# A two-layer hybrid transformer trunk on one core: where TensorE computes the modulation rows

## The reference

```
mx = (silu(c) @ w_mod[i] + b_mod[i])          # w_mod[i] is 1024 x 6144, six rows of 1024
sh1, sc1, g1, sh2, sc2, g2 = split(mx, 6)
x = x + g1 * mixer(modulate(rms_norm(x, norm1_g[i]), sh1, sc1))
x = x + g2 * moe_ffn(modulate(rms_norm(x, norm2_g[i]), sh2, sc2), ...)
```

## Time and profile before

| | |
|---|---|
| median of 3 runs | 909.59 us |
| profiled execution | 907.71 us, span 905.8 us |
| TensorE busy | 833.9 us (92%), 6940 products |
| VectorE, ScalarE, GpSimd busy | 406.6, 241.3, 93.1 us |
| DMA | 300.59 MB, mean 332 GB/s |
| chain that ended last | TensorE 66%, DMA 17%, VectorE 8% |
| mean granted TensorE clock | 0.961 |
| one VectorE addition of 128x512 (line 1459) | 689 ns |

### The profile page before, as it was taken

One profiled execution on the slowest core, in us unless ns is written; L12 is line 12 of the kernel. 1 busy time (PEld: TensorE's weight loads), 2 busy tenths in 40 slices (PEclk: granted clock), 3 DMA queues, 4 the chain that ended last, 5 costly groups with the idle time before them and its releaser, 6 DMA issues.

```text
span 905.8 us, 16815 instructions
## 1 busy us (share of the span) xinstructions
PE 833.9 (92%) x6940; PEld 520.8 (57%) x6940; DVE 406.6 (45%) x674; ACT 241.3 (27%) x449; POOL 93.1 (10%) x162
## 2 busy tenths in 40 slices
PE   5898999999999799999996999989899899998994
PEld 2588995596646355553543887467555355453541
DVE  0468998737422222332336643466622232332334
ACT  3742435613211011111103523343111111110112
POOL 4184000012000000000000254100000000000000
PEclk9999999997999799999997999999999899999998
DMA  9999996848999999989997986596999999989993
GB/s 357 367 259 295 333 355 192 289 164 286 368 392 397 392 397 391 389 274 399 394 398 294 328 240 184 172 382 225 385 391 397 389 398 393 392 304 393 392 397 131
DMA packets 142158, 300.59 MB, mean 332 GB/s; under 512 B 12576, under 2 KB 43584, under 8 KB 142072
## 3 DMA queue, kind: packets, MB, share of 16 engines
q1 hardware_dynamic: 135360, 286.53, 87.5%
q0 software_dynamic: 6384, 12.76, 4.9%
q10 hardware_dynamic: 328, 0.11, 0.0%
HBM read 291.77 MB, written 2.92 MB: 325 GB/s over the span
## 4 chain that ended last, share of the span: by engine, by line
PE 66%; DMA 17%; DVE 8%; issue 3%; ACT 3%; SPq 2%; DVEq 0%; ACTq 0%
PE ps L2016 20%; DMA ring<-in_moe_w 11%; PE ps L2041 11%; PE ps L1969 4%; DMA ring<-in_w_mod 4%; PE ps L2106 3%; PE ps L1939 3%; DMA ring<-in_na_w_in 2%; PE ps L1940 2%; PE ps L1620 2%; PE ps L2132 2%; PE ps L2134 2%; PE ps L2133 2%; SPq L621 2%; DVE wlo L1106 2%
## 5 line engine op out<-in xcount | busy, mean ns | idle before, releaser
L2016 PE MATMUL ps<-ring,xg 128*64 128x256 f32 (+1 forms) x2432 | 255.3, 394 | 11.1 <-DMA ring<-in_moe_w 9.7
L2016 PEld LDWEIGHTS ps<-ring,xg 128*64 128x64 f32 (+1 forms) x2432 | 134.3, 130 | 103.2 <-issue 41.2
L1475 DVE SCALAR_TENSOR_TENSOR xres<-ps,gs,xres 128x512 f32<-128x512 f32 x128 | 90.0, 747 | 188.4 <-PE ps L1969 188.4
L2041 PE MATMUL ps<-ring,hidT 128*64 128x512 f32 (+1 forms) x608 | 121.8, 607 | 7.5 <-DMA ring<-in_moe_w 6.7
L2041 PEld LDWEIGHTS ps<-ring,hidT 128*64 128x64 f32 (+1 forms) x608 | 33.0, 129 | 76.6 <-issue 63.2
L1106 DVE TENSOR_TENSOR wlo<-ring,whi 128x1024 fp32r<-128x1024 f32 x56 | 66.6, 1219 | 12.8 <-ACT whi L807 12.8
L807 ACT CAST whi<-ring 128x1024 fp32r<-128x1024 f32 x56 | 56.8, 1045 | 53.0 <-DMA ring<-in_na_w_in 37.0
L1459 DVE TENSOR_TENSOR yg<-ps,g2keep 128x512 f32<-128x512 f32 x32 | 21.5, 689 | 82.7 <-PE ps L2041 82.7
L1620 PE MATMUL ps<-ring,pair 128*32 128x256 f32 x576 | 45.6, 436 | 12.6 <-DMA ring<-in_w_mod 7.7
L974 ACT COPY xg<-ps 128x384 f32<-128x384 f32 (+2 forms) x44 | 20.7, 470 | 130.7 <-PE ps L1940 130.7
L1939 PE MATMUL ps<-pick,hthi 128*128 128x192 f32 (+1 forms) x192 | 50.3, 302 | 0.0
(11 more groups left out here) (265 smaller groups left out, 1323.7 us busy)
## 6 DMA issues: line engine op xcount, KB each, us to landing
ring<-in_moe_w SPq DMA_DIRECT2D x384, 512.0 KB, 11.7
ring<-in_w_mod SPq DMA_DIRECT2D x96, 512.0 KB, 7.3
ring<-in_na_w_in SPq DMA_DIRECT2D x24, 512.0 KB, 8.7
ring<-in_cf_pw_w SPq DMA_DIRECT2D x24, 512.0 KB, 8.4
ring<-in_ab_w_out SPq DMA_DIRECT2D x8, 512.0 KB, 4.9
mods<-mod_scratch POOLq DMA_DIRECT2D x8, 512.0 KB, 7.1
urep<-uT SPq DMA_DIRECT2D x64, 35.5 KB, 3.5
urep<-uT POOLq DMA_DIRECT2D x64, 35.5 KB, 3.4
```

Source lines behind the costliest of these rows:

```text
L1475: V.scalar_tensor_tensor(out=dst, in0=ps[:, plan.spread_banks(m, i)[half], :], scalar=gs[:, t, place:place + 1], in1=dst, op0=ALU.mult, op ...
L2016: ins = T.matmul(ps[lo:lo + width, BW[a], c0:c0 + 2 * P], tile[:, k, o:o + width], raw[:, p.slot(u), w0:w0 + 2 * P], start=(q == 0 and kk ...
L2041: ins = T.matmul(ps[lo:lo + width, BY[a], :], hidT[:, a, o:o + width], raw[:, p.slot(u), half * HALF:(half + 1) * HALF], start=(q == 0), s ...
```

## The change

The arithmetic stays as it is; the order does not.

- `FIRST`: the 24 units of modulations 5, 6 and 7 stand among the output projection's 8 units, three ahead of each, instead of 16 among them and 8 behind. In the attention TensorE takes one unit in even turns and two in odd ones. Bank 7 holds modulation 7.
- `SECOND`: modulation 9 stands behind the second unit of pw2, ahead of the next four; 10 and 11 behind these; the last two units of pw2 at the end. TensorE takes modulation 9 (into bank 1) ahead of pw1's last block, and all of 10 and 11 behind the last convolution, ahead of pw2. The last piece of `cuts` is 8 units instead of 4.
- No modulation is left to take at the start of `experts`.
- VectorE's row sums move along: 5 and 6 into attention turns 8 and 13, 7 to the first mix, 9 ahead of the norm's sums, 10 ahead of pw2's mixes, 11 among them. GpSimd's row moves of 5 and 6 and its load of the second layer's bias rows go ahead of its wait for the scores.
- The mask is added by VectorE, at the points of the weight order that `MASK_AT` gives, instead of by GpSimd.
- The first item of a stage waits for the first gathered half ahead of step 0 and for the second ahead of step 2.

```diff
@@ -105,8 +105,7 @@
     w("in", NA, NA)
     among([("in", 2 * NA, NA), ("in", 0, NA), ("in", 3 * NA + SC, SC), ("in", 3 * NA + 2 * SC, SC), ("in", 3 * NA, SC)],
           SUMMED, lambda i: min(24, max(0, 3 * (i - 2) // 2)))
-    among([("out", 0, D)], (5, 6), lambda i: 2 * i)
-    mod(7)
+    among([("out", 0, D)], (5, 6, 7), lambda i: 3 * i)
     return out
 
 
@@ -122,7 +121,7 @@
         pw1.extend(("w", "pw1", D + c, h) for h in range(DENSE))
         pw2.extend(("w", "pw2", c, h) for h in range(DENSE))
     mod = lambda v: [("mod", v, k) for k in range(KC)]
-    return mod(8) + pw1 + pw2[:SPL] + mod(9) + mod(10) + pw2[SPL:] + mod(11)
+    return mod(8) + pw1 + pw2[:2] + mod(9) + pw2[2:SPL] + mod(10) + mod(11) + pw2[SPL:]
 
 
 FIRST = first_stream()
@@ -666,7 +665,7 @@
                         eng.dma_start(urep[s * QUAD:(s + 1) * QUAD, ch % 3, g, :],
                                       uT[g * QUAD:(g + 1) * QUAD, ch, s:s + REP]).then_inc(rep_in[ch % 3], 16)
 
-            cuts = [0, 22, 26, 30, 34]
+            cuts = [0, 22, 26, 30, 38]
             for j in range(4):
                 load_dense(SECOND[cuts[j]:cuts[j + 1]], SECOND_U + cuts[j])
                 replicate(2 * j)
@@ -739,22 +738,15 @@
 
             for h in range(HEADS):
                 load_bias(h)
-            eng.wait_ge(small_in, 48)
-            for h in range(HEADS):
-                eng.wait_ge(bias_in[h], 64)
-                full = bias[:, h].rearrange("p t (r c) -> p (t r) c", r=ROWS)
-                mask = cst[:, C_MASK:C_MASK + GRID_W].unsqueeze(1).broadcast_to([P, NT * ROWS, GRID_W])
-                nc.gpsimd.tensor_tensor(full, full, mask, ALU.add).then_inc(bias_masked, 1)
-            for v in range(2, 5):
+            for v in range(2, 6):
                 mod_move(v)
+            eng.dma_start(quads(bmr[:]), b_mod[1].rearrange("(v q n) -> q v n", v=6, q=4)).then_inc(mod_bias_in, 16)
+            mod_move(6)
 
             eng.wait_ge(scores, 2 * HEADS)
             for v in range(2, 5):
                 mod_fill(v, mods[:, v * D:(v + 1) * D])
-            mod_move(5)
-            eng.dma_start(quads(bmr[:]), b_mod[1].rearrange("(v q n) -> q v n", v=6, q=4)).then_inc(mod_bias_in, 16)
             gate_fill(5)
-            mod_move(6)
 
             def mod_next(v):
                 mod_fill(v, mods[:, (v - 6) * D:(v - 5) * D])
@@ -1124,12 +1116,23 @@
                     V.scalar_tensor_tensor(out=acc[:], in0=raw_unit(u), scalar=pair[:, k, 0:1], in1=acc[:],
                                            op0=ALU.mult, op1=ALU.add).then_inc(unit_done, 1)
 
+            def mask_bias(h):
+
+                if h == 0:
+                    eng.wait_ge(small_in, 48)
+                eng.wait_ge(bias_in[h], 64)
+                full = bias[:, h].rearrange("p t (r c) -> p (t r) c", r=ROWS)
+                mask = cst[:, C_MASK:C_MASK + GRID_W].unsqueeze(1).broadcast_to([P, NT * ROWS, GRID_W])
+                V.tensor_tensor(full, full, mask, ALU.add).then_inc(bias_masked, 1)
+
             def upto(k):
 
                 while nw[0] < k:
                     if FIRST[todo[0]][0] == "mod":
                         mod_add(todo.pop(0))
                         continue
+                    for h in MASK_AT.get(nw[0], ()):
+                        mask_bias(h)
                     rest_dense(todo.pop(0), nw[0])
                     nw[0] += 1
                     if nw[0] - 1 in SUM_AFTER:
@@ -1278,8 +1281,8 @@
                 if n % 2 == 0 and n <= 12:
                     upto(24 + n // 2)
                 normalised(n)
-                if n == 2:
-                    mod_sum(4)
+                if n in (2, 8, 13):
+                    mod_sum({2: 4, 8: 5, 13: 6}[n])
                 if n % 4 == 2 and n > 2:
                     hp = n // 4 - 1
                     eng.wait_ge(a_rounded, hp + 1)
@@ -1307,9 +1310,7 @@
                     upto(32)
                 mix(n, PROJ["out"], g1, ytmp)
                 if n == 0:
-                    mod_sum(5)
-                if n == 5:
-                    mod_sum(6)
+                    mod_sum(7)
                 if n == 6:
                     mod_filled(eng, 4)
                     eng.wait_ge(x_mixed, 7)
@@ -1324,7 +1325,6 @@
                 for t in range(NT):
                     modulated(htok, t, mods[:, 3 * D:4 * D])
 
-                mod_sum((7, 11)[L])
                 for t in range(NT):
                     eng.wait_ge(ht_rounded, 2 * L + t + 1)
                     V.tensor_tensor(htlo[:, t, :], htok[:, t, :], hthi[:, t, :], ALU.subtract).then_inc(ht_rest, 1)
@@ -1556,6 +1556,7 @@
                 stack(2 * j)
                 stack(2 * j + 1)
 
+            mod_sum(9)
             wide = [P, 2, SEQ]
             eng.wait_ge(ln_sum, 1)
             total, squared = ps[:, 0, 0:SEQ], ps[:, 0, SEQ:2 * SEQ]
@@ -1575,7 +1576,7 @@
                 eng.wait_ge(s_rounded, q + 1)
                 V.tensor_tensor(sTlo[:, 2 * q:2 * q + 2, :], sT[:, 2 * q:2 * q + 2, :], sThi[:, 2 * q:2 * q + 2, :],
                                 ALU.subtract).then_inc(s_rest, 1)
-            mod_sum(9)
+            mod_sum(10)
             eng.wait_ge(pw2b_in, 16)
             mod_filled(eng, 8)
             for n in range(8):
@@ -1583,7 +1584,7 @@
                     rest_second(W_SECOND)
                 mix(n, PROJ["pw2"], mods[:, 2 * D:3 * D], ytmp2, pbB)
                 if n == 1:
-                    mod_sum(10)
+                    mod_sum(11)
                 if n == 6:
                     mod_filled(eng, 10)
                     eng.wait_ge(x_mixed, 15)
@@ -1852,7 +1853,7 @@
                         ins = T.transpose(ps[:, n % 2, q * P:(q + 1) * P], prob[:, n % 2, q * P:(q + 1) * P], ident)
                     ins.then_inc(prob_T, 1)
                 if n < 16:
-                    mods_before(FIRST.index(("mod", 7, 0)), 1)
+                    mods_before(len(FIRST), 1 + n % 2)
                 if n == 16:
                     eng.wait_ge(a_rest, 3)
                     out_part(0, (0, 1, 2), False, False)
@@ -1893,7 +1894,6 @@
 
             def experts(L):
 
-                mods_before(len(FIRST) if L == 0 else len(FIRST) + len(SECOND))
                 for t in range(NT):
                     eng.wait_ge(h_set, 4 * L + t + 1)
                     for a in range(2):
@@ -1998,7 +1998,9 @@
                         width = SLOTS // len(it.places)
                         for s in range(8):
                             between(m, s)
-                            if s == 0:
+                            if it.batch == 0 and s % 2 == 0 and s < 4:
+                                p.wait(eng, "g_taken", ready[0] - 1 + s // 2)
+                            elif s == 0:
                                 p.wait(eng, "g_taken", ready[it.batch])
                             name, q = ("w1", "w3")[s // 4], s % 4
                             c0 = s // 4 * 2 * P
@@ -2116,6 +2118,8 @@
 
             done_n = SECOND_W
             for j in range(4):
+                if j == 3:
+                    mods_before(SECOND_U + SECOND.index(("mod", 10, 0)))
                 if j == 2:
                     eng.wait_ge(mod_row, 7)
                     eng.wait_ge(cols_set, 4)
@@ -2148,7 +2152,7 @@
             conv(7)
             channel_sums(6)
             channel_sums(7)
-            mods_before(SECOND_U + SECOND.index(("mod", 10, 4)))
+            mods_before(SECOND_U + len(SECOND))
             npj = 0
             for b in range(4):
                 eng.wait_ge(unit_done, done_count(SECOND_AT[done_n - SECOND_W + 1]))
@@ -2158,8 +2162,6 @@
                     dst = ps[:, npj % 4, 0:BLOCK]
                     for k in range(KC):
                         if npj == 0 and k % 2 == 0:
-                            if k:
-                                mods_before(SECOND_U + SECOND.index(("mod", 11, 0)), 1)
                             eng.wait_ge(s_rest, k // 2 + 1)
                         a0, a1 = sThi[:, k, t * P:(t + 1) * P], sTlo[:, k, t * P:(t + 1) * P]
                         T.matmul(dst, a0, wpart2(done_n, k, 0, 0, BLOCK), start=(k == 0), stop=False)
@@ -2167,8 +2169,6 @@
                         ins = T.matmul(dst, a1, wpart2(done_n, k, 0, 0, BLOCK), start=False, stop=(k == KC - 1))
                         if t == NT - 1 and k == 3:
                             ins.then_inc(w_used, 1)
-                        if npj == 1 and k == 3:
-                            mods_before(SECOND_U + SECOND.index(("mod", 11, 0)), 1)
                     ins.then_inc(w_used if t == NT - 1 else proj, 1)
                     npj += 1
                 done_n += DENSE
@@ -2180,11 +2180,12 @@
 GAINS = (4, 7, 10)
 
 SUM_AFTER = {13: 2, 21: 3}
+MASK_AT = {8: (0, 1, 2), 9: (3, 4), 10: (5,), 12: (6,), 14: (7,)}
 
 
 def mod_bank(v):
 
-    return 6 + v % 2 if v < 7 else BX[v % 2]
+    return 1 if v == 9 else 6 + v % 2 if v < 8 else BX[v % 2]
 
 
 OUT_BANKS = [4, 5, 2, 3, 0, 1, 2, 3]
```

## The result

| | before | after |
|---|---|---|
| median | 908.01 us, 4 runs (906.34 to 909.95) | 927.24 us, 4 runs (922.52 to 931.75) |
| ratio, 95% interval | | 1.021 (1.0146 to 1.0275) |
| profiled execution | 907.71 us, span 905.8 | 931.75 us, span 929.9 |
| mean granted TensorE clock | 0.961 | 0.939 |

The forecast was 911 with a range of 899 to 920, and "no difference" as the likeliest. The time lies outside the range, on the slow side. The ratios of the experiments leave out three slow executions, 922.83 and 1179.46 us of e13 with 42 and 922.75 us of e14.

What follows compares the result with a forecast made beforehand. Dense stages were taken as bound by TensorE, VectorE and ScalarE, expert-stage starts by late weights. Layer 0's -5.3 and layer 1's +7.4 summed to +2.1 us on 907.7 profiled, written as 911 median, range 899 to 920.

Steps and rivals of the forecast that it cites:

- Attention, +1.9: Layer 0 attention: eight extra modulation units in odd turns lengthen eight turn pairs by 0.24 us each, 1.9 us in all.
- half wait: First turn of each expert stage: waiting only for the first gathered half saves 0.7 us in each layer.
- mask 0: Mask additions moved from GpSimd to VectorE: no effect on the time, bounds -4.0 and +0.7 us.
- Expert stage, layer 0, -9.0: Expert stage of layer 0: a 7.1 us lead of weight transfers clears nine waits and half clock, saving 9.0 us.
- Empty gap, layer 0, +2.5: Idle TensorE ahead of layer 0's router: the clock falls to half for transposes and router products, costing 2.5 us.
- Modulation 9, +9.1 and +1.5: Ahead of the last gating block: modulation 9 with late units takes 9.1 us, half clock behind it 1.5 us.
- Norm's gap, 0: Norm's gap ahead of pw2 in layer 1: modulations 10 and 11 there cost nothing, bounds -1 and +3 us.
- Empty gap, layer 1, +3.0: Idle TensorE ahead of layer 1's router: half clock for router products and part of the transposes costs 3.0 us.
- Expert stage, layer 1, -5.5: Expert stage of layer 1: a 4.6 us transfer lead against waits and half clock saves 5.5 us.
- Rival (a): Both expert stages: waits shrink only by 4 and 3 us and the clock still dips; about 919 us, chance 0.22.
- Rivals (b) to (d): (b) clock keeps, stages clear: 904, 0.22; (c) modulation 9 lands in time: 906, 0.12; (d) attention starves: 916, 0.09.

Runs made afterwards that it cites:

- e13 with 42: Full change with all of modulation 9 and four units of modulation 10 issued ahead of convolution copies, plus five idle products in layer 1's emptied gap: 913.84 us.
- e14: Full change with all of modulation 9 issued ahead of the copies for convolutions 4 and 5, plus five idle products in layer 1's emptied gap: 913.90 us.
- e1: Kernel before with only the layer-0 part: modulation 7 among the output weights and taken in the attention; 905.59 us, ratio 0.9961.
- e10: Full change without its layer-1 part, plus five idle products at the start of layer 0's expert stage: 905.18 us, ratio 0.9973 against before.
- e7: Kernel before with only modulation 9 moved ahead of the last gating block: 922.45 us, ratio 1.0142.
- e9: Full change with all eight units of modulation 9 issued ahead of the copies for convolutions 4 and 5: 919.59 us, ratio 1.0117 against before.
- e12: Full change plus five idle products at the start of layer 1's expert stage alone: 916.39 us, ratio 1.0098 against before.
- e8: Kernel before with modulations 9, 10 and 11 all in the norm's gap, none at the expert stage: 924.48 us, ratio 1.0193.
- e13 with 46: Full change with all of modulations 9 and 10 issued ahead of convolution copies, plus five idle products in layer 1's emptied gap: 923.93 us.
- e2: Kernel before with only the layer-1 part: modulation 9 ahead of the last gating block, 10 and 11 in the norm's gap; 926.10 us, ratio 1.0182.

## Why the prediction was wrong

*Attention, +1.9 (measured +1.0), half wait, mask 0:* right. The half wait's 0.68 us is gone in both layers of after; it was not run alone.

*Expert stage, layer 0, -9.0:* mis-sized. -3.5 in the profile, and e1 as a whole gives -3.5 us. Even my lower bound, -4.9, was too much. I took the lead as the time from issue to landing less that of an empty queue (11.0 - 3.9); it left out that a full ring stops the queue, which gave 5.9 us back by the estimate above. That this is the reason is read from the traffic and not tested by a run.

*Empty gap, layer 0, +2.5:* unclear by size. The clock fell as forecast. The router's products took 6.85 us at half clock in four profiles and 3.9 in four, but idle products there (e10) brought nothing.

*Modulation 9, +9.1 and +1.5:* the mechanism (four late units, 4.8 us of waiting, half clock) is the one seen; its size was 11.0 and 1.9. e7 puts the step at +12.9 though it relieves the norm's gap; e9 and e14 (against e12) put what hangs on the place of one cut in SP's queue at 8.4 and 5.1 us.

*Norm's gap, 0:* this step failed. It counted the eight units of modulation 10 as landed when the gap begins. SP issued them from 585.81 on, when the copies had gone out, in one run with those of 11; four had landed when the gap began, and TensorE waited for the rest from 599.04 at 1.28 us each until 613.6. I had expected the last unit 14.5 us after the convolutions, and its products began 17.5 us after (596.1 to 613.6), at half clock. e7, after and e8 together show that units over the dozen that the norm hides cost their transfer or more, and e13 with 46 that it is the late ones that cost.

*Empty gap, layer 1, +3.0:* this step failed too, beyond its bound of 4.4. I priced only the transposes and the router at half clock. The clock also stayed down through most of the gather; the stretch to the first expert product grew by 5.7 us. Idle products give back 6.8 to 10.2 us (e14 against e9, e12 against the full change), more than that stretch; the rest came in the expert stage, which opened at full clock in after and in e12 and had its stretches at half clock later, at its waits for weights, and what links these to the gap is open. Why the clock was slower to come back here in after, e2 and e9 than in e8 is open too. The pieces in which TensorE ran in the norm's gap don't explain it: the mean clock there was 0.71 in after and 0.60 in e8, and between the two gaps TensorE worked for 22.9 us at a mean of 0.95.
The Trainium skill (TensorE: Matmul & The Clock Gate, HAM oscillation) has the wall-time price of a throttled stretch as half its length. Here the mean clock of 0.56 over 25.8 us means some 22.7 us at 1.2 GHz, so 11.4 us by that rule, an estimate, and the 0.90 of e12's 17.7 us means 3.5 us and 1.8: 9.6 us apart by the rule, 8.1 measured. The rule comes out within a fifth, and my length of the stretch was wrong. That an array which waited too long starts the next burst throttled, as the prediction took from the same section, the traces bear out: behind each of the twelve idle gaps of 4.26 or 4.72 us the transposes took 3.16 us or more, not 2.29.

*Expert stage, layer 1, -5.5:* +1.6 in the profile of after, 247.0 us against 250.3 before, so -3.3, in e12. The lead gives about its lower bound, -2.7, with idle products (247.0 to 249.1 us) and less than 1 us without (249.4 to 251.9). Its 4.6 us are given back in the first 10 us of the stage, while the ring is full (208 GB/s against 399); this term left out the full ring as that of layer 0 did.

Of the 22 us between forecast and profile, 12.6 are gains of the two stages that did not come (5.5 and 7.1) and 12.2 are prices set too low (norm's gap 5.3, modulation 9 3.5, emptied gap 3.4), less 2.8 of small errors the other way. Rival (a), "the stages don't give what the lead promises", was the case, but its 919 left the other costs at their forecast. Rivals (b) to (d) fell: the clock did not keep, the units were late, and the attention did not starve. A slip of the chances: (a) and (d) alone make the 0.31 for slower, so nothing is left in it for the forecast's upper edge.

## To carry to other kernels

Work that stands in a gap may be what keeps the clock: before moving it out, price everything that follows at half clock until the next long dense stretch, not only the next group of products, and consider idle products in its place. Repeat such a measurement, since the clock comes back early in some executions and late in others. A gap that hides a statistics chain also has a transfer budget; count the units that have landed by SP's issue times, not by where they stand in the order, and see what else the queue must send there. A lead on a ring of slots seems to be worth at most what the ring holds, less the time for which it stands full; here that was an estimate from the traffic.

## What the runs showed of the hardware

- Five idle products (ten in the trace's count), 4.45 us in a gap of 4.9, kept the granted clock at 1.00 through the next 5.7 us (e12). With the 4.72 us left idle it was 0.50 through the next 10.3 us in after, e2 and e9; in e8 it was 0.50 for 3.7 us and back for the router's products.
- Behind idle time of 4.26 us (layer 0) the 16 transposes took 3.16 to 3.67 us in all eight profiles that have it, against 2.29 without such a gap, and the router's products behind them took 3.9 us in four and 6.85 us in four, with nothing between. A single profile can't price such a gap.
- Modulation units land at 1.28 us each when the queue is full, with 390 GB/s moved; 0.52 MB a unit at that rate would be 1.34 us.
- With the eight 512 KB units of modulation 10 issued ahead of them, the 16 small copies of e13 with 46 began at 579.18, and a convolution waited for them for 11 us; with four of these ahead (e13 with 42) it waited 3.72 us, and with none of them (after, e9) not at all.
